# The last layer's down projection as seven block products a step, with up in half steps

## The reference

```python
        x = _layer_norm(DEEPNORM_ALPHA * x + y, ln1_g[layer], ln1_b[layer])
        h = jnp.square(jax.nn.relu(jnp.einsum('bsd,df->bsf', x, w_ff1[layer])))
        y = jnp.einsum('bsf,fd->bsd', h, w_ff2[layer])
        x = _layer_norm(DEEPNORM_ALPHA * x + y, ln2_g[layer], ln2_b[layer])
```

## Time and profile before

| | before |
|---|---|
| median of 3 runs | 1482.01 us (1481.84 to 1482.99) |
| the profiled execution's own time | 1481.5 us |
| its span in the profile | 1479.7 us |
| granted TensorE clock, mean | 0.999 of full speed |
| last feed-forward, from its second up on | 1305.22 to 1471.08 us of the span |

### The profile page before, as it was taken

How to read it: one execution, slowest core, us unless ns; L and a number is a source line. 1 busy time by engine, 2 the same in 40 slices (tenths; PEclk the granted TensorE clock), 3 DMA queues, 4 the chain that set the end, 5 groups by cost and what they waited for, 6 DMA issues and landing times.

```text
span 1479.7 us, 18304 instructions
## 1 busy us (share of the span) xinstructions
PE 1469.1 (99%) x7446; PEld 1240.0 (84%) x7446; DVE 1155.7 (78%) x1159; ACT 853.6 (58%) x855; POOL 153.8 (10%) x160
## 2 busy tenths in 40 slices
PE   9999999999999999999999999999999999999997
PEld 8878888888888888888888888888998888888886
DVE  7899877799998999877676799986785566875565
ACT  6666666666666666654344666666455575454343
POOL 0000210200002000033030200002011200010000
PEclk9999999999999999999999999999999999999999
DMA  9898554589859698565535689855444435464551
GB/s 369 262 307 279 182 199 175 216 278 274 287 167 328 208 300 270 171 225 182 181 133 197 267 244 293 277 172 206 160 164 156 145 140 182 151 236 174 200 195 57
DMA packets 47748, 318.46 MB, mean 215 GB/s; under 512 B 5696, under 2 KB 6144, under 8 KB 10928
## 3 DMA queue, kind: packets, MB, share of 16 engines
q1 hardware_dynamic: 38592, 270.35, 48.6%
q0 software_dynamic: 7264, 43.19, 13.3%
q10 hardware_dynamic: 1808, 3.74, 0.7%
HBM read 282.60 MB, written 1.05 MB: 192 GB/s over the span
## 4 chain that ended last, share of the span: by engine, by line
PE 96%; DMA 2%; DVE 2%; ACT 0%; issue 0%; POOLq 0%; POOL 0%; SPq 0%; DVEq 0%
PE psum L2036 16%; PE psum L2040 16%; PE psum L2039 16%; PE psum L2145 7%; PE psum L2282 6%; PE psum L2286 6%; PE psum L2283 6%; PE psum L2172 5%; PE psum L2149 4%; PE psum L2179 3%; PE psum L2068 2%; PE psum L2081 2%; PE psum L2074 2%; DMA ln_rows<-normalised 1%; PE psum L2048 1%; PE psum L2374 1%
## 5 line engine op out<-in xcount | busy, mean ns | idle before, releaser
L1206 DVE TENSOR_TENSOR weights_lo<-weights_raw,weights_hi 128x2048 fp32r<-128x2048 f32 x183 | 422.2, 2308 | 178.0 <-ACT weights_hi L634 176.4
L634 ACT ACTIVATE weights_hi<-weights_raw 128x2048 fp32r<-128x2048 f32 (+1 forms) x190 | 357.5, 1881 | 210.7 <-PE psum L2040 128.5
L2036 PE MATMUL psum<-weights_hi,hidden_hi 128*128 128x512 f32 x416 | 164.1, 394 | 0.9 <-DVE weights_lo L1206 0.9
L2039 PE MATMUL psum<-weights_lo,hidden_hi 128*128 128x512 f32 x416 | 162.4, 390 | 0.0
L2040 PE MATMUL psum<-weights_hi,hidden_lo 128*128 128x512 f32 x416 | 162.2, 390 | 0.0
L2036 PE MATMUL psum<-weights_hi,operand 128*128 128x512 f32 x384 | 151.5, 394 | 0.0
L2039 PE MATMUL psum<-weights_lo,operand 128*128 128x512 f32 x384 | 149.9, 390 | 0.0
L2040 PE MATMUL psum<-weights_hi,operand 128*128 128x512 f32 x352 | 137.2, 390 | 0.0
L1206 DVE TENSOR_TENSOR weights_lo<-weights_raw_more,weights_hi 128x2048 fp32r<-128x2048 f32 x52 | 118.8, 2285 | 4.6 <-ACT weights_hi L634 4.6
L634 ACT ACTIVATE weights_hi<-weights_raw_more 128x2048 fp32r<-128x2048 f32 x52 | 99.5, 1916 | 2.3 <-DMA weights_raw_more<-weights_raw 1.9
L2145 PE MATMUL psum<-operand,weights_hi 128*128 128x512 f32 x416 | 99.0, 390 | 0.0
(11 more groups left out here) (407 smaller groups left out, 2988.0 us busy)
## 6 DMA issues: line engine op xcount, KB each, us to landing
weights_raw<-in_weights SPq DMA_DIRECT2D x174, 1024.0 KB, 4.9
weights_raw_more<-in_weights SPq DMA_DIRECT2D x60, 1024.0 KB, 9.6
weights_raw<-weights_raw POOLq DMA_DIRECT2D x12, 1024.0 KB, 12.2
normalised<-in_weights SPq DMA_DIRECT2D x12, 1024.0 KB, 4.8
ln_rows<-in_weights SPq DMA_DIRECT2D x8, 1024.0 KB, 10.4
weights_raw_more<-ln_rows POOLq DMA_DIRECT2D x8, 1024.0 KB, 7.4
ln_rows<-in_ln_rows POOLq DMA_DIRECT2D x16, 512.0 KB, 5.8
ln_rows<-normalised POOLq DMA_DIRECT2D x4, 1024.0 KB, 16.3
```

What stands on the lines that cost most here:

```text
L634: nc.scalar.activation(hi[:, rest], whole[:, rest], ACT.Copy).then_inc(hi_split, 1)
L1206: nc.vector.tensor_tensor(lo_of(n), raw_of(n), hi_of(n).bitcast(F32), ALU.subtract).then_inc(lo_split, 1)
L2036: mm(out, a_hi, b_hi, start=start, stop=False, skip_group_check=True)
L2039: mm(out, a_hi, b_lo, start=False, stop=False, skip_group_check=True)
```

## The change

The layer's down projection is cut into 2 x 2 x 2 blocks a step: two token halves, two halves of the step's hidden features (256 each), two column halves of 512. Steps 0 to 6 are computed from seven products instead of eight. The weight operands are the raw blocks b11, b21, b22 and the sums t1 = b11 + b12, t2 = b22 + t1, t3 = t2 - b11, t4 = b21 + t2; t1, t2 and t4 are made in the raw tile by DMAs that POOL issues (`add_block_t1`, `_t2`, `_t4`), t3 by DVE. The hidden operands are three blocks and four sums, which DVE makes (`part_form_sums`). Each of the seven products adds up through the seven steps in a PSUM bank of its own; so both halves of up (256 features each, `up_half`) share the eighth bank, and their matmuls all have 256 columns. Step 7 is multiplied plainly (`plain`). The seven banks are put together in the residual and in `acc` around layer norm 8, by DVE, ACT and POOL.

Operands become half tiles: eight half slots instead of three whole ones, and eight raw slots. Each half tile is split by its own instruction on ACT; DVE splits two halves of up at once where their slots lie side by side. Loads keep their size (1 MB) and number.

The diff, cut to its core:

```diff
+def ff2_operands():
+    up = lambda s, half: [("up", s, half, part) for part in range(2)]
+    operands, last = [("up", 0, 0, 0), ("up", 0, 1, 0)] + up(1, 0) + up(1, 1) + up(2, 0), FF2_STEPS - 1
+    early, late = ("b22", "b11", "t1", "b21"), ("t2", "t3", "t4")
+    for s in range(last - 2):
+        operands += [(b, s) for b in early] + up(s + 2, 1) + [(t, s) for t in late] + up(s + 3, 0)
+    operands += [(b, last - 2) for b in early] + up(last, 1) + [("b22", last - 1)] + [(t, last - 2) for t in late]
+    return operands + [(b, last - 1) for b in early[1:] + late] + [(b, last) for b in ("p11", "p12", "p21", "p22")]
...
+        if n == N_HALVES:
+            used = [k for k in used for part in range(2)]
+        if n >= N_HALVES:
+            s = min(range(2 * OPERAND_SLOTS), key=lambda k: used[k])
...
+            def add_block_t1(s):
+                b11, t1 = FF2_AT["b11", s], FF2_AT["t1", s]
+                pool.wait_ge(weight_loaded[RAW_SLOT[LOAD_OF[t1]]], RAW_COUNT[LOAD_OF[t1]])
+                pool.dma_start(raw_of(t1), raw_of(b11), accum_op=ALU.add).then_inc(t1_added, 16)
+            def add_block_t2(s):
+                t1, t2 = FF2_AT["t1", s], FF2_AT["t2", s]
+                pool.wait_ge(t1_added, 16 * (4 * len(GROUPS) + s + 1))
+                pool.wait_ge(lo_split, FF2_AT["b22", s] + 1)
+                pool.dma_start(raw_of(t2), raw_of(t1), accum_op=ALU.add).then_inc(t2_added, 16)
+            def add_block_t4(s):
+                t2, t4 = FF2_AT["t2", s], FF2_AT["t4", s]
+                pool.wait_ge(t2_added, 16 * (s + 1))
+                pool.wait_ge(lo_split, FF2_AT["b21", s] + 1)
+                pool.dma_start(raw_of(t4), raw_of(t2), accum_op=ALU.add).then_inc(t4_added, 16)
+            for s in range(FF2_STEPS - 1):
+                add_block_t1(s)
+                add_block_t2(s)
+                add_block_t4(s)
+            u, v = in_pair(gate_up[:, 0:2, :]), in_pair(gate_up[:, 2:4, :])
+            pool.wait_ge(products_summed, 3)
+            pool.wait_ge(act_kept, 4)
+            nc.gpsimd.tensor_tensor(resid[:, 1, 0:NCOL], resid[:, 1, 0:NCOL], u, ALU.add).then_inc(resid_ready, 1)
+            nc.gpsimd.tensor_tensor(resid[:, 1, NCOL:], resid[:, 1, NCOL:], v, ALU.add).then_inc(resid_ready, 1)
             layer_norm(8)
             pool.wait_ge(last_scaled, 1)
...
+            for s in range(last - 2):
+                if s:
+                    relu_half(s + 2, 0)
+                whole_up_hi(s + 2, 1)
+                if not s:
+                    second_parts_hi(1)
+                    part_forms_hi(1)
+                    relu_half(s + 2, 0)
+                block_hi("t2", s)
+                first_part_hi(s + 2)
+                block_hi("t3", s)
+                block_hi("t4", s)
+                relu_half(s + 2, 1)
+                whole_up_hi(s + 3, 0)
+                block_hi("b22", s + 1)
+                block_hi("b11", s + 1)
+                second_parts_hi(s + 2)
+                block_hi("t1", s + 1)
+                part_forms_hi(s + 2)
...
                         dve.wait_ge(weights_used, end)
+                        if ln == 8:
+                            dve.wait_ge(resid_ready, 2 * 8 + 2)
+                    elif (ln, tb, b) == (8, 1, 0):
+                        dve.wait_ge(resid_ready, 2 * 8 + 1)
+                        dve.wait_ge(weights_used, FF2_AT["p21", FF2_STEPS - 1] + 1)
                     else:
...
+                        if (ln, tb, b) == (8, 0, 1):
+                            product_sums()
...
+            def add_block_t3(s):
+                b11 = raw_of(FF2_AT["b11", s])
+                dve.wait_ge(t2_added, 16 * (s + 1))
+                nc.vector.tensor_tensor(b11, raw_of(FF2_AT["t2", s]), b11, ALU.subtract).then_inc(tile_added, 1)
+            def square_half(s, half):
+                dve.wait_ge(ff2_relu, 2 * (s - 1) + half + 1)
+                dve.wait_ge(ff2_ready, 3 * s - 1)
+                dve.wait_ge(ff2_summed, s)
+                nc.vector.tensor_tensor(hid_rows(half), from_rows(in_pair(gate_up[:, 2 * half:2 * half + 2, :])), from_rows(up_bank(s, half)),
+                                        ALU.mult).then_inc(ff2_squared, 1)
...
+                f0, f1, f2 = (squares[:, k * TOK:(k + 1) * TOK] for k in (1, 2, 3))
+                first = mark(nc.vector.tensor_tensor(squares[:, 0:NCOL].rearrange("p (b t) -> p b t", b=2),
+                                                     hid[:, 1:2, :].to_broadcast([P, 2, TOK]), hid[:, 0:4:3, :], ALU.subtract))
+                dve.wait_ge(dve_step, first)
+                third = mark(nc.vector.tensor_tensor(f1, f0, hid[:, 0, :], ALU.subtract))
+                dve.wait_ge(dve_step, third)
+                nc.vector.tensor_tensor(f2, hid[:, 2, :], f1, ALU.add).then_inc(ff2_summed, 1)
...
+            def first_product_sum():
+                dve.wait_ge(resid_ready, 2 * 8)
+                dve.wait_ge(act_kept, 3)
+                nc.vector.tensor_tensor(resid[:, 0, 0:NCOL], work[:, 0, :], resid[:, 0, 0:NCOL], ALU.add)
+            def fourth_product_less():
+                dve.wait_ge(weights_used, FF2_AT["t3", FF2_STEPS - 2] + 1)
+                nc.vector.tensor_tensor(resid[:, 1, 0:NCOL], resid[:, 1, 0:NCOL], acc[:, 3, :], ALU.subtract).then_inc(act_kept, 1)
+            def product_sums():
+                u, v = in_pair(gate_up[:, 0:2, :]), in_pair(gate_up[:, 2:4, :])
+                nc.vector.tensor_tensor(u, work[:, 1, :], u, ALU.add).then_inc(products_summed, 1)
+                dve.wait_ge(products_summed, 1)
+                nc.vector.tensor_tensor(v, work[:, 2, :], u, ALU.subtract).then_inc(products_summed, 1)
+                dve.wait_ge(products_summed, 2)
+                nc.vector.tensor_tensor(resid[:, 0, NCOL:], resid[:, 0, NCOL:], v, ALU.add).then_inc(products_summed, 1)
+                dve.wait_ge(products_summed, 3)
...
+            for s in range(last - 2):
+                if s:
+                    square_half(s + 2, 0)
+                up_lo(s + 2, 1)
+                if not s:
+                    second_parts_lo(1)
+                    part_form_sums(1)
+                    part_forms_lo(1)
+                    square_half(s + 2, 0)
+                add_block_t3(s)
+                block_lo("t2", s)
+                first_part_lo(s + 2)
+                block_lo("t3", s)
+                block_lo("t4", s)
+                square_half(s + 2, 1)
+                up_lo(s + 3, 0)
+                block_lo("b22", s + 1)
+                part_form_sums(s + 2)
+                block_lo("b11", s + 1)
+                second_parts_lo(s + 2)
+                block_lo("t1", s + 1)
+                part_forms_lo(s + 2)
+                block_lo("b21", s + 1)
...
+            def up_half(s, half, between=None):
+                for part in range(2):
+                    n = FF2_AT["up", s, half, part]
+                    w_hi_n, w_lo_n = hi_of(n), lo_of(n)
+                    if part and between:
+                        between()
+                    blocks = [(4 * part + k, b, slice(k * TOK + b * P, k * TOK + (b + 1) * P)) for k in range(4) for b in range(2)]
+                    out = lambda b: up_bank(s, half)[:, b * TOK:(b + 1) * TOK]
+                    pe.wait_ge(hi_split, n + 1)
+                    for c, b, cols in blocks:
+                        mm(out(b), w_hi_n[:, cols], x_hi[:, c, :], start=c == 0 and b == 0, stop=False, skip_group_check=True)
+                        mm(out(b), w_hi_n[:, cols], x_lo[:, c, :], start=False, stop=False, skip_group_check=True)
+                    pe.wait_ge(lo_split, n + 1)
+                    for c, b, cols in blocks:
+                        last = mm(out(b), w_lo_n[:, cols], x_hi[:, c, :], start=False, stop=c == KC - 1, skip_group_check=True)
+                    last.then_inc(weights_used, 1)
+            ff2_banks = {"b11": work[:, 0, :], "t2": work[:, 1, :], "t1": work[:, 2, :],
+                         "b21": acc[:, 0, :], "b22": acc[:, 1, :], "t4": acc[:, 2, :], "t3": acc[:, 3, :]}
+            ff2_part = {"b11": (first_at, 0, 1), "b21": (second_at, 0, 2), "t4": (second_at, 1, 2),
+                        "t3": (forms_at, 0, 3), "t1": (forms_at, 1, 3), "t2": (forms_at, 2, 3), "b22": (forms_at, 3, 3)}
+            def block(what, s):
+                n, out = FF2_AT[what, s], ff2_banks[what]
+                part_of, k, count = ff2_part[what]
+                w_hi_n, w_lo_n = hi_of(n), lo_of(n)
+                a_hi, a_lo = part_hi(part_of(s) + k), part_lo(part_of(s) + k)
+                chunks = [(slice(c * P, (c + 1) * P), slice(c * NCOL, (c + 1) * NCOL)) for c in range(2)]
+                pe.wait_ge(ff2_ready, 3 * s + count)
+                pe.wait_ge(hi_split, n + 1)
+                for c, (rows, cols) in enumerate(chunks):
+                    mm(out, a_hi[:, rows], w_hi_n[:, cols], start=s == 0 and c == 0, stop=False, skip_group_check=True)
```

(36 more changed lines are left out.)

303 lines of the change are left out of this document (227 added, 76 removed).

## The result

The kernel after takes **1489.44 us** (median of 5 runs, 1488.17 to 1490.24), the kernel before 1481.84: a ratio of **1.0051**, 95% interval 1.0041 to 1.0062. It is 7.6 us slower; 1476.3 us was forecast. Two executions among all the runs (2316.72 us of the kernel before, 7491.05 us in experiment 10) ran at a granted clock of 0.594 and 0.184 and stand in no ratio.

The account below looks back on a forecast made before the run. PE was taken to bound the kernel (busy 1469.1 of 1479.7 us). Down -9.55, up +2.7 and the end +1.2 gave -5.7 us, so the median 1482.0 becomes 1476.3 us; range 1473.5 to 1485.

Parts of the forecast that it names:

- PE's work: Last feed-forward: fewer down matmuls -9.55 us, narrower up matmuls +2.7 us, together -6.9 us; a step 21.04 us.
- The walk: One step of the last feed-forward traced across PE, ACT and DVE: no stall follows, smallest margin 1.2 us.
- DVE at 87%: DVE's work in a step of the last feed-forward, summed to 18.2 of 21.04 us, which fits beside PE.
- DVE's chain binds: Rival: DVE's tight margin before up makes PE wait up to 1 us a step; 1478 to 1484 us; chance 19%.
- the margin of up's low half: In the walk, the low part of up (s+3, 0) is ready 1.2 us before PE wants it.
- The end: Behind the last products, DVE takes the last bank 1.2 us later behind PE than before: +1.2 us, bounds 0 and +2.2.
- The adding DMAs: Half-tile adds for t1, t2, t4 on POOL's queue, taken at 5 us a piece: no stall.
- The lone half: An add of half a tile (0.5 MB) with nothing beside it should land in about 4.4 us.
- the loop, 7.5 us and two adds: From t2's add to the next step's t2 add: t2's and t4's adds plus 7.5 us of ACT and DVE work.
- the bound of 13.5: The loop fits in a step of 21.04 us while its two adds take under 13.5 us, 6.8 each.
- The adds become the loop: Rival: two adds over 13.5 us lengthen each of five loops by the excess; most between 1484 and 1500 us; chance 15%.
- its price formula: In that rival, each of five loops is longer by what its two adds exceed 13.5 us; at 9.4 a piece, +27 in all.

Follow-up runs that it names:

- experiment 10: Kernel of experiment 8 with DVE's first new sum (u = p + t2's bank) moved ahead of the last half tile's split; run twice: 1480.27 and 1479.94 us.
- experiment 6: Changed kernel whose last 24 weight loads bring only 128 of 2048 columns, adds and waits untouched; 1478.24 us, ratio 0.9976.
- experiment 1: Changed kernel without the 21 adding DMAs for t1, t2, t4; those products use plain halves; 1476.68 us, ratio 0.9964.
- experiment 9: Changed kernel with nine held loads as meant: four wait for the t2 add right behind their split, five for t4's; 1487.85 us, ratio 1.0041.
- experiment 4: Changed kernel with t2 and t4 added by POOL instructions instead of DMAs, t1 still by DMA; 1497.43 us, ratio 1.0106.
- experiment 2: Changed kernel with one more wait: the next step's t1 add isn't issued before t4's add has landed; 1489.33 us, ratio 1.0052.
- experiment 3: Changed kernel with five loads held until t4's add has landed, steps 0 to 4; 1484.04 us, ratio 1.0016.
- experiment 5: Kernel of experiment 3 with four more loads held for t2's add, by mistake the t2 add of a step later; 1498.76 us, ratio 1.0115.
- experiment 7: Changed kernel with product b22 of step s+1 moved ahead of t4 of step s on ACT, DVE and PE; 1482.95 us, ratio 1.0007.
- experiment 8: Kernel of experiment 7 with POOL also issuing t1's add of step s+1 ahead of t4's of step s; 1479.97 us, ratio 0.9987.
- experiment 11: Kernel before with 21 more adding DMAs of 8 columns on POOL that no other engine waits for; 1483.25 us, ratio 1.0008.

## Why the prediction was wrong, step by step

- **PE's work** was right. Up parts last 2.88 us, 11.52 a step (11.49 taken), a product 1.36 us. By the timelines PE's last matmul starts at 1470.67 before (the chain of waits puts that piece at 1470.84) and at 1464.61 without adds: 6.1 us less for the 6.9 of the sum; the other 0.8 isn't placed.
- **The walk and DVE at 87%** were right. Without adds, PE has no wait in the last layer, and DVE is busy 18.3 of 21 us in the middle stretches (18.2 summed). "DVE's chain binds" had no part in the result. It was the margin of up's low half, 1.2 us in the walk, that was used up first when an add was late: the waits of 0.7 us stand there.
- **The end** was right as far as it went: by the timelines the last bank is taken 1.37 us behind PE instead of 0.28, 1.1 more for the 1.2 summed. Wrong by omission: 1.5 us behind the last instruction, which no row of the trace before could give, since it showed one count of DMAs alone.
- **The adding DMAs: the step that failed.** The lone half was right, 4.4 us forecast and 4.4 to 4.5 measured; so were the loop, 7.5 us and two adds, to 0.3 us, and the bound of 13.5. The failed sentence is "I take 5 us a piece, near the lone row, since the loads come in bursts of one or two". Measured for t2 and t4 of steps 0 to 4: a mean of 7.2 us, single ones up to 10.4, all of those over 8 beside loads. I had worked out 7.0 and 9.4 from the earlier trace rows myself and kept the most favourable value, against rows at 12.2 and 17.0 us. In the walk I had also let t2's add meet one load and t4's none. In fact one add's delay reached the other: in steps 1 and 3, with t2's add slow, t4's started late, near the next loads (SP issues one at 1351.36, 0.2 us behind t4's at 1351.16), and was slow too, 8.5 + 9.8 in step 1; in steps 2 and 4, with t2's fast, t4's ran ahead of them, 6.0 + 4.5. Step 0 is the exception: t2's took 10.4 us, but the next load was issued only at 1335.18, 4.2 us behind t4's add, which took 4.5.
- **"The adds become the loop"** was the case that came, with 15% where it should have had the most, and its price formula held. One thing in it was wrong: "it breaks even at about 7.4 us a piece". The measured mean was 7.2, and still 10 us were lost, because a step gives PE nothing back when its adds are short (loops of 18.0 and 17.8 us still took over 20), and costs most of the excess when they are long (26.1 - 21.0 = 5.1, twice; PE lost 4.1 and 4.2 us at them), and the clock on top.
- **The clock** wasn't in the forecast at all: 1.6 us behind a wait of 3.54 us.

The sum of it: 1476.3 forecast, 1476.7 without adds (5.0 us under the kernel before that was run beside it, where 5.7 was summed). With them the span is 11.5 us longer (1486.2 to 1474.7): 9.9 us up to PE's last matmul, and 1.6 behind it. Matching PE's matmuls of the two profiles one by one places the 9.9: 4.1 at the first wait, 1.6 by the clock, 3.2 at the second, 1.0 at the third, 0.4 near 1464 us, less 0.3 that PE was ahead when the layer began. So the three listed waits (3.5 + 2.5 + 0.7) cost 1.5 us more than their length: the first matmuls behind a long wait start 0.30 us apart (1362.16, 1362.46) instead of 0.23, and the low passes start late again. The medians differ by 12.8, since the profiled execution lies 1.3 us under its median.

The one add by itself: the Trainium skill ("DMA: Bandwidth & Descriptors", section "Anatomy of one DMA — SWDGE (gpsimd) path") has a fixed 2 us and the bytes at 436 GB/s for a DMA of POOL's queue. By that page an estimate for 512 KB is 3.2 us. The adds here took 4.4 or 4.5 us, 11 of the 21 of experiment 6. The measurement decides; by the page's figure the adds would have seemed to fit more easily still.

## What to carry to other kernels

A transfer that depends on another, with an engine in order behind it, belongs in a loop that is written down with its slowest landings and not with a mean or a lone one: short rounds give nothing back. If the sum doesn't fit, move the work that gates the next transfer ahead of the wait (here one product, five places, and two issues: 9.5 us), instead of delaying the loads, which only picks another victim. And a free engine is only free if it doesn't share what the busy one needs.

## What the runs showed of the chip

- An accumulating DMA of 512 KB within on-chip memory lands in 4.4 to 4.5 us alone, in some 5 to 14.7 beside loads of 1 MB and other adds, and in 16.1 to 18.0 in the burst of loads at the layer's start. A load of 1 MB takes longer beside adds too: 4.7 us alone in experiment 1, 6.5 beside t4's add in experiment 9.
- Each adding DMA on POOL's queue adds about 0.07 us between POOL's last instruction and the end of the span, 8 columns or 1024: 5.24 us in the kernel before, 5.72 with 7 more (experiment 4), 6.74 to 6.81 with 21 more (the kernel after and experiments 2, 3 and 5 to 11).
- A POOL addition of two SBUF operands holds a DVE operation with all its operands in SBUF that starts behind it until it ends (2.51 us instead of 0.42). Six DVE operations with one operand in PSUM kept their 0.68 us beside it, though only one of them started behind POOL's.
- PE's clock fell to 1.2 GHz for over 3 us after 3.54 us without work, and not after 2.5 us; in experiment 5 it fell after 3.7 and 4.0 us, and not after 3.0. The length of one wait isn't the whole of it: in experiment 4 it fell twice for 3.4 us, after waits of 1.9 us (1355.67, with one of 0.6 us some 5 us ahead) and 2.3 us (1468.20), and not after three others of 1.9.
